# The end of a two-block transformer kernel: the last residual addition done by accumulating transfers into DRAM

## The chip, the cores and the metric

The kernel runs on one core of a Trainium2 chip. The metric is device time in microseconds (us) of one execution. A core has five engines that run their own instruction streams and meet only at semaphores: TensorE (PE, matrix products into PSUM banks), VectorE (DVE) and ScalarE (ACT) for elementwise work, GpSimd (POOL), and SyncE (SP), which here only issues transfers (DMAs). A DMA moves data between DRAM and the on-chip memory SBUF. It can be issued by SP, ACT or POOL, and is carried out by 16 DMA engines that all of them share.

## The reference

Two blocks run one after the other on a sequence of 512 tokens with 1024 channels. What matters here is the very end of the second block, the feed-forward part:

```python
def reference(x, ...):
    x = first_block(x, ...)
    return second_block(x, ...)

def second_block(x, ...):
    h = x
    for l in range(DEPTH_2):            # one layer
        a = rms_norm(h, ln_mix_pre[l])
        ...                             # four mixers side by side
        mix = jnp.concatenate([y_a, y_b, y_c, y_d], axis=-1) @ w_out[l]
        h = h + rms_norm(mix, ln_mix_post[l])

        a = rms_norm(h, ln_ffn_pre[l])
        ff = (jax.nn.silu(a @ w_ffn_gate[l]) * (a @ w_ffn_up[l])) @ w_ffn_down[l]
        h = h + rms_norm(ff, ln_ffn_post[l])
    return h
```

The output is `h + rms_norm(ff, ...)`: a residual `h` that is known before the feed-forward part begins, plus `ff` scaled by one number per token and one per channel.

## The kernel before, in words

Activations lie transposed: channels on the 128 partitions, in 8 tiles `k` of 128 channels, and the 512 tokens along each row. `X` holds the residual (128 x 8 x 512, f32, 2 MB), `Y` the output of the last product. Every product is done in three f32 passes (high and low halves of weights and activations), so PE is busy nearly all the time: weights stream from DRAM in units of up to 512 KB (SP, `load`, L1308), ACT makes their high half (`high`, L1321), DVE their low half (`low`, L1327), PE multiplies (L1446 to L1448).

The last stage is `feed_forward` (L3786). Its parts run in this order on PE: the output product of the mixers, gate/up product of the first half of the hidden channels, down product of that half, then the same two for the second half. The first product is followed by the norm object `mixed`, the last by `final`; both are of the class `RmsPost` (L1071). `mixed` computes `X = X + norm(Y)` and the halves for the next product; it ends with X holding the last residual `h`. `final` computes `X = X + norm(Y)` again, which is the output.

How `RmsPost` works for `final`. As each block of the down product is added into `Y` (`block`, and L336), ACT squares it (L1121), and POOL sums the squares (L1128, L1131). The last of the 8 blocks is computed in two halves of 256 tokens (`in_halves`, L1462): PE finishes the first half and increments the semaphore `half`, then does the second half and increments `unit_used`. Between its last products PE forms the mean of the squares of each token with a matrix of constants (L1091, L1097), and ACT turns it into the inverse root, by a logarithm and an exponential (L268, L269), in the tile `line[INV]`, whose semaphore `inv` reaches 2 when the first half of the tokens is done and 4 with the second.

DVE runs `dve_last` (L1172). `norm(i)` is two instructions: Y times channel gain times inverse root (L1187, scalar_tensor_tensor), and X plus that (L1189, tensor_tensor). The items `i` of `final` are 13 pieces: 5 tiles of the first 256 tokens, 5 of the second, and 3 tiles of all 512 tokens. DVE does the first half of block 8 (L1177), waits for `inv` 2, does two items, then `whole()` (a wait for PE to end), the second half of block 8 (L1177), and the rest, with a wait for `inv` 4 before item 5. ACT needs that second L1177 for the square that the second half's inverse root begins with.

The output is stored by `store` (L1215): for every item a wait for its addition, and one DMA from X to `out`, the even items by SP and the odd ones by ACT. Each then waits for its own transfers to land, and the program ends.

Of the kernel before, what the change touches and what calls it, by code (L numbers as in the profile page):

```python
# [10 lines left out]
ALU = mybir.AluOpType  # L11
# [4 lines left out]
T = 512  # L16
# [183 lines left out]
class Stage:  # L200
# [34 lines left out]
    def block(self, pool=None):  # L235


        block = self.ctx.enter_context(self.nc.Block(no_gpsimd_drain=True))
        self.cleared, self.core.to_clear = self.core.to_clear, []

        @block.gpsimd
        def _(eng):
            nums = sorted(h.num for h in self.cleared)
            while nums:
                n = 1
                while n < len(nums) and nums[n] == nums[0] + n:
                    n += 1
                eng.sem_clear(range(nums[0], nums[0] + n))
                nums = nums[n:]
            if pool:  # L250
                pool(eng)
        return block
# [569 lines left out]
class LayerNorm:  # L822
# [106 lines left out]
    def pool(self, gp):  # L929
        core, s, Y, line = self.core, self.s, self.core.Y, self.core.line  # L930
        self.tile_ready(gp, 1)
        done(gp, gp.tensor_tensor(line[SUM][:], Y[:, 0, :], Y[:, 1, :], ALU.add), s.sum)  # L932
        gp.wait_ge(s.sq, 2)
        done(gp, gp.tensor_tensor(line[SSUM][:], line[SQ0][:], line[SQ1][:], ALU.add), s.ssum)
        for k in range(2, KD - 1):
            self.tile_ready(gp, k)
            done(gp, gp.tensor_tensor(line[SUM][:], line[SUM][:], Y[:, k, :], ALU.add), s.sum)
            gp.wait_ge(s.sq, k + 1)
            done(gp, gp.tensor_tensor(line[SSUM][:], line[SSUM][:], line[(SQ0, SQ1)[k % 2]][:], ALU.add), s.ssum)
# [131 lines left out]
class RmsPost:  # L1071
# [100 lines left out]
    def dve_last(self, dve, evac, whole, split):  # L1172
        core, s, X, Y, line = self.core, self.s, self.core.X, self.core.Y, self.core.line

        def block(h):
            i, cols = self.b0 + KD - 1 + h, HALVES[h]
            dve.tensor_tensor(Y[:, KD - 1, cols], Y[:, KD - 1, cols], core.bank(i)[:, cols], ALU.add).then_inc(core.freed(i), 1)  # L1177

        def low(i):
            k, cols = self.items[i]  # L1180
            dve.wait_ge(s.src_hi, i + 1)
            dve.scalar_tensor_tensor(self.xl[:, k, cols], X[:, k, cols], core.param(self.pre, k), self.xh[:, k, cols].bitcast(F32),  # L1182
                                     ALU.mult, ALU.subtract).then_inc(s.src_lo, 1)

        def norm(i):
            k, cols = self.items[i]
            dve.scalar_tensor_tensor(Y[:, k, cols], Y[:, k, cols], core.param(self.post, k), line[INV][:, cols], ALU.mult, ALU.mult).then_inc(s.normed, 1)  # L1187
            dve.wait_ge(s.normed, i + 1)
            dve.tensor_tensor(X[:, k, cols], X[:, k, cols], Y[:, k, cols], ALU.add).then_inc(s.x, 1)  # L1189

        if self.restored:
            dve.wait_ge(self.restored, 16)
        dve.wait_ge(s.half, 1)
        if isinstance(evac, Accumulate):
            block(0)
        split()
        dve.wait_ge(s.inv, 2)
        begun = 3 if self.late else 2
        for i in range(begun):
            norm(i)  # L1200
            if self.late and i:
                low(i - 1)
        whole()
        if isinstance(evac, Accumulate):
            block(1)
        for i in range(begun, len(self.items)):
            if self.items[i] == (0, HALVES[1]):
                dve.wait_ge(s.inv, 4)
            norm(i)
            if self.late:  # L1210
                low(i - 1)
        if self.late:
            low(len(self.items) - 1)

    def store(self, eng, odd, sem):  # L1215
        out = self.core.io["out"].rearrange("p (k t) -> p k t", t=T)
        for i in range(odd, len(self.items), 2):
            k, cols = self.items[i]
            eng.wait_ge(self.s.x, i + 1)
            eng.dma_start(out[:, k, cols], self.core.X[:, k, cols]).then_inc(sem, 16)  # L1220
        eng.wait_ge(sem, 16 * len(range(odd, len(self.items), 2)))

# [2561 lines left out]
def feed_forward(core):  # L3786


    with Stage(core, "ffn") as st:
        x, h = core.source, core.hidden[FT]  # L3790
        s = st.sems("restored stored_sp stored_act")
        mixed = RmsPost(core, st, "a", "post", x, "fpre", restored=s.restored)
        final = RmsPost(core, st, "b", "fpost")
        parts = [Product(core, st, "out_", KD, (KD,), [(KD, Plain(core.Y))], Split(st, core.Y, x), mixed)]
        for half in range(2):
            up = Gated(*h, mixed)
            parts.append(Product(core, st, f"gateup{half}_", 2 * FT, (KD,), [(2 * FT, up)], mixed if half == 0 else Hidden(x)))
            out = Plain(core.Y) if half == 0 else Accumulate(core.Y)
            parts.append(Product(core, st, f"down{half}_", KD, (6, 5), [(KD, out)], Hidden(h, up.s.hidden_lo), final if half else None))

        def pool(gp):
            mixed.pool(gp)
            final.pool(gp)

        def restore(act):
            act.dma_start(core.X[:], core.io["kept"].rearrange("p (k t) -> p k t", t=T)).then_inc(s.restored, 16)

        def sync(sp):
            final.store(sp, 0, s.stored_sp)

        def scalar_last(act):
            final.store(act, 1, s.stored_act)

        Chain(core, st, parts).run(st, pool=pool, sync=sync, scalar_first=restore, scalar_last=scalar_last)


def program(nc, io):
    with ExitStack() as ctx:
        core = Core(nc, io, ctx)
        for n, kts, blocks in STREAMS:  # L3820
            for i in range(blocks * len(kts)):
                kt = kts[i % len(kts)]
                core.stream.append((io[n][i][:, 0:kt * P], kt))
        place = lambda n, shape, at: nc.alloc_sbuf_tensor_at(n, shape, F32, offset=at)
        Z, O = place("Z1", [P, 27, T], Z1_AT), place("O", [P, KD, T], LINE_AT(4))
        small, norm = core.Y[:, 4:7, :], place("rwkv_norm", [P, 4, T], LINE_AT(0))
        gate = place("rwkv_gate", [P, 4, T], end_of("W") - 4 * TILE)

        AR = place("rwkv_AR", [P, 4, NCH, 2, C], at_of("S"))
        elast = place("rwkv_elast", [P, 4, NCH], at_of("H") + 4 * TILE)  # L3830
        load_and_project(core, Z, O, small, norm, gate, AR, elast)
        rwkv(core, Z, O, gate, AR, elast)
        first_layers(core, O)
        dilated_layer(core)
        Z, gates = place("Z2", [P, 16, T], at_of("H")), place("gates", [P, 1, T], LINE_AT(INV))
        made = LateInputs(core)
        second_layers(core, Z, gates, made)
        late_mixers(core, Z, gates[:, 0, :], made)
        feed_forward(core)
# [112 lines left out]
```

## Time and profile before

| | us |
|---|---|
| median of 3 runs (lowest, highest) | 2152.04 (2150.08, 2152.43) |
| the profiled execution's own time | 2155.46 |
| its span, first to last instruction | 2153.7 |
| PE busy / DVE busy / ACT busy / POOL busy | 2078.1 / 1233.9 / 822.8 / 274.2 |

The profiled execution was 3.4 us longer than the median of the timed runs; 1.8 us of its time lie outside its span. PE is busy 96% of the span, at a granted clock of 0.991 of full speed. An engine's busy time does not tell what the end waits for: for a change at the very end, the instructions of the last 20 us have to be read in order, engine by engine. In rows of the timeline the first number is the start of an instruction in us, the second its duration.

### The profile page before, as it was taken

The page shows a single profiled execution, that of the slowest core. Times are in us where ns is not written, and L with a number is a line of the kernel's source. Part 1 is how long each engine was busy: PE and PEld are TensorE (multiplying, and loading weights), DVE is VectorE, ACT ScalarE, POOL GpSimd, SP SyncE. Part 2 cuts the span into 40 slices and gives each one's busy share as a digit, 9 for nine tenths or more (in the row PEclk, how much of TensorE's full clock was granted, in tenths as well). Part 3 has the DMA queues.
Part 4 walks back from the last instruction along what each step waited for, and adds up shares of the span by engine and source line. Part 5 has one row for each costly group of instructions (what it writes and reads, how often), then busy time and mean ns, then how long its engine had stood idle before and what let it go on. Part 6 is the DMA issues. An engine that isn't in the chain of part 4 may idle for free. (4 is left out here: it accounts for less than half of the span.)

```text
span 2153.7 us, 31656 instructions
## 1 busy us (share of the span) xinstructions
PE 2078.1 (96%) x12976; PEld 1680.8 (78%) x12976; DVE 1233.9 (57%) x1760; ACT 822.8 (38%) x1317; POOL 274.2 (13%) x262
## 2 busy tenths in 40 slices
PE   8999989999999999999999999999998899999997
PEld 6876868888888878888888888886665578888886
DVE  5558866642444676667473553467678647533544
ACT  4343234531332534444462332353234554322322
POOL 0000003000002100000301870030542010000001
PEclk9999999999999999999999999999999999999999
DMA  6220003333223222222123222223111042233322
GB/s 234 69 71 27 4 3 108 98 98 98 90 96 98 70 93 74 69 71 77 59 88 103 89 98 98 98 93 122 59 59 36 2 147 88 91 90 114 98 81 66
DMA packets 52400, 179.29 MB, mean 83 GB/s; under 512 B 5864, under 2 KB 7144, under 8 KB 52000
## 3 DMA queue, kind: packets, MB, share of 16 engines
q1 hardware_dynamic: 48144, 165.58, 23.7%
q10 hardware_dynamic: 3616, 8.00, 1.1%
q0 software_dynamic: 496, 3.69, 0.4%
q8 instruction: 103, 1.69, 0.3%
q14 instruction: 41, 0.34, 0.1%
HBM read 172.51 MB, written 4.21 MB: 82 GB/s over the span
## 5 line engine op out<-in xcount | busy, mean ns | idle before, releaser
L1332 DVE TENSOR_TENSOR w_lo<-w_raw,w_hi 128x1024 fp32r<-128x1024 f32 (+1 forms) x320 | 402.6, 1260 | 664.1 <-ACT w_hi L1325 657.2
L1325 ACT ACTIVATE w_hi<-w_raw 128x1024 fp32r<-128x1024 f32 (+1 forms) x320 | 328.9, 1031 | 800.3 <-PE banks L1448 744.2
L1446 PE MATMUL banks<-xh,w_hi 128*128 128x512 f32 x1544 | 617.6, 400 | 3.6 <-PEq L214 2.6
L1448 PE MATMUL banks<-xh,w_lo 128*128 128x512 f32 x1544 | 603.7, 391 | 0.0
L1447 PE MATMUL banks<-xl,w_hi 128*128 128x512 f32 x1544 | 603.2, 391 | 0.0
L1446 PEld LDWEIGHTS banks<-xh,w_hi 128*128 128x128 f32 x1544 | 291.1, 189 | 73.3 <-issue 13.1
L1448 PEld LDWEIGHTS banks<-xh,w_lo 128*128 128x128 f32 x1544 | 290.5, 188 | 62.0
L1447 PEld LDWEIGHTS banks<-xl,w_hi 128*128 128x128 f32 x1544 | 291.2, 189 | 57.4 <-issue 1.2
L1446 PE MATMUL banks<-hh,w_hi 128*128 128x512 f32 x653 | 255.2, 391 | 1.0 <-DVE hl L372 1.0
L1447 PE MATMUL banks<-hl,w_hi 128*128 128x512 f32 x653 | 254.4, 390 | 0.0
L1448 PE MATMUL banks<-hh,w_lo 128*128 128x512 f32 x653 | 254.3, 389 | 0.0
L1446 PEld LDWEIGHTS banks<-hh,w_hi 128*128 128x128 f32 x653 | 122.6, 188 | 27.3 <-DVE hl L372 1.4
L1447 PEld LDWEIGHTS banks<-hl,w_hi 128*128 128x128 f32 x653 | 122.6, 188 | 25.8 <-issue 0.5
L1448 PEld LDWEIGHTS banks<-hh,w_lo 128*128 128x128 f32 x653 | 122.6, 188 | 25.4
L932 POOL TENSOR_TENSOR line<-Y 128x512 f32<-128x512 f32 x4 | 5.2, 1294 | 1068.6 <-DVE Y L915 1068.6
L1128 POOL TENSOR_TENSOR line<-line,line 128x512 f32<-128x512 f32 x2 | 2.6, 1290 | 421.0 <-ACT line L1121 421.0
L1507 PE MATMUL banks<-xh,w_hi 128*128 128x256 f32 (+1 forms) x165 | 53.3, 339 | 1.8 <-ACT xh L961 1.3
L1508 PE MATMUL banks<-xh,w_lo 128*128 128x256 f32 (+1 forms) x165 | 52.1, 332 | 0.0
L372 DVE TENSOR_TENSOR hl<-line,hh 128x512 fp32r<-128x512 f32 x64 | 48.4, 757 | 2.2
L369 DVE TENSOR_TENSOR line<-line 128x512 f32<-128x512 f32 x64 | 48.3, 755 | 0.0
L361 ACT ACTIVATE hh<-line 128x512 fp32r<-128x512 f32 x64 | 40.6, 635 | 2.0
L1514 PE MATMUL banks<-xl,w_hi 128*128 128x256 f32 (+1 forms) x165 | 39.7, 349 | 1.5 <-DVE xl L1029 0.6
(540 smaller groups left out, 2770.2 us busy)
## 6 DMA issues: line engine op xcount, KB each, us to landing
w_raw<-in_w SPq DMA_DIRECT2D x128, 512.0 KB, 3.5
w_raw<-in_w_gu SPq DMA_DIRECT2D x44, 512.0 KB, 3.5
w_raw<-in_w_c_in SPq DMA_DIRECT2D x40, 512.0 KB, 3.5
w_raw<-in_w_ab_in SPq DMA_DIRECT2D x27, 512.0 KB, 3.5
w_raw<-in_w_in SPq DMA_DIRECT2D x25, 512.0 KB, 3.4
w_raw<-in_w_down SPq DMA_DIRECT2D x16, 384.0 KB, 3.1
w_raw<-in_w_down SPq DMA_DIRECT2D x16, 320.0 KB, 2.8
w_raw<-in_w_ab_out SPq DMA_DIRECT2D x8, 512.0 KB, 3.5
```

Of the source, the lines that this page charges most:

```text
L361: act.activation(self.hh[:, b, :], relu[:], ACT.Square).then_inc(self.s.hidden_hi, 1)
L369: dve.tensor_tensor(sq[:], relu[:], relu[:], ALU.mult).then_inc(self.s.squared, 1)
L372: dve.tensor_tensor(self.hl[:, b, :], sq[:], self.hh[:, b, :].bitcast(F32), ALU.subtract).then_inc(self.s.hidden_lo, 1)
L932: done(gp, gp.tensor_tensor(line[SUM][:], Y[:, 0, :], Y[:, 1, :], ALU.add), s.sum)
L1325: act.activation(core.w_hi[u % SLOTS][:, 0:n], core.raw[u % RAW][:, 0:n], ACT.Copy).then_inc(core.hi_ready, 1)
L1332: dve.tensor_tensor(lo[:, 0:n], core.raw[u % RAW][:, 0:n], hi[:, 0:n].bitcast(F32), ALU.subtract).then_inc(core.split_ready, 1)
L1446: pe.matmul(bank, hi[:, w], src.xh[:, kk, :], start=kk == 0, stop=False)
L1447: pe.matmul(bank, hi[:, w], src.xl[:, kk, :], start=False, stop=False)
L1448: mm = pe.matmul(bank, lo[:, w], src.xh[:, kk, :], start=False, stop=last)
L1507: pe.matmul(banks[i][:, cols], hi[:, w], src.xh[:, k, cols], start=n == 0, stop=False, skip_group_check=True)
L1508: pe.matmul(banks[i][:, cols], lo[:, w], src.xh[:, k, cols], start=False, stop=False, skip_group_check=True)
L1514: mm = pe.matmul(banks[i][:, cols], hi[:, w], src.xl[:, k, cols], start=False, stop=last, skip_group_check=True)
```

## The change

`mixed`, the norm in front of the feed-forward products, now has a `store` too: once all its items are added (X holds the last residual), POOL issues one transfer of the whole of X, 2 MB, to `out`. At the end, `norm(i)` of `final` is only the scaling L1187; the addition L1189 is left out. For every item POOL waits until it is scaled and issues a DMA from Y to `out` with `accum_op=ALU.add`: the transfer adds Y to what lies in DRAM. `final.add` first waits for the earlier store (`stored`), and at the end for all 13 transfers. SP and ACT store nothing. In `dve_last` the wait `whole()` and the second half of block 8 now come before all items of `final`, in place of after two.

```diff
         def norm(i):
             k, cols = self.items[i]
             dve.scalar_tensor_tensor(Y[:, k, cols], ...).then_inc(s.normed, 1)
-            dve.wait_ge(s.normed, i + 1)
-            dve.tensor_tensor(X[:, k, cols], X[:, k, cols], Y[:, k, cols], ALU.add).then_inc(s.x, 1)
+            if self.late:
+                dve.wait_ge(s.normed, i + 1)
+                dve.tensor_tensor(X[:, k, cols], X[:, k, cols], Y[:, k, cols], ALU.add).then_inc(s.x, 1)
...
         split()
+        if not self.late:
+            whole()
+            block(1)
         dve.wait_ge(s.inv, 2)
-        begun = 3 if self.late else 2
+        begun = 3 if self.late else 0
...
-        whole()
-        if isinstance(evac, Accumulate):
-            block(1)
+        if self.late:
+            whole()
...
-    def store(self, eng, odd, sem):
+    def store(self, gp, sem):
         out = self.core.io["out"].rearrange("p (k t) -> p k t", t=T)
-        for i in range(odd, len(self.items), 2):
-            k, cols = self.items[i]
-            eng.wait_ge(self.s.x, i + 1)
-            eng.dma_start(out[:, k, cols], self.core.X[:, k, cols]).then_inc(sem, 16)
-        eng.wait_ge(sem, 16 * len(range(odd, len(self.items), 2)))
+        gp.wait_ge(self.s.x, len(self.items))
+        gp.dma_start(out, self.core.X[:]).then_inc(sem, 16)
+
+    def add(self, gp, stored, sem):
+        out = self.core.io["out"].rearrange("p (k t) -> p k t", t=T)
+        gp.wait_ge(stored, 16)
+        for i, (k, cols) in enumerate(self.items):
+            gp.wait_ge(self.s.normed, i + 1)
+            gp.dma_start(out[:, k, cols], self.core.Y[:, k, cols], accum_op=ALU.add).then_inc(sem, 16)
+        gp.wait_ge(sem, 16 * len(self.items))
...
         def pool(gp):
             mixed.pool(gp)
+            mixed.store(gp, s.stored)
             final.pool(gp)
+            final.add(gp, s.stored, s.added)
...
-        Chain(core, st, parts).run(st, pool=pool, sync=sync, scalar_first=restore, scalar_last=scalar_last)
+        Chain(core, st, parts).run(st, pool=pool, scalar_first=restore)
```

The end of DVE's stream before, from the last whole block of the down product (L336) on; the first L1177 is the first half of block 8, line_56 is the inverse root:

```order
L336 TENSOR_TENSOR Y<-Y,banks 128x512
L1177 TENSOR_TENSOR Y<-Y,banks 128x256
L1187 SCALAR_TENSOR_TENSOR Y<-Y,params,line_56 128x256
L1189 TENSOR_TENSOR X<-X,Y 128x256
L1187 SCALAR_TENSOR_TENSOR Y<-Y,params,line_56 128x256
L1189 TENSOR_TENSOR X<-X,Y 128x256
L1177 TENSOR_TENSOR Y<-Y,banks 128x256
L1187 SCALAR_TENSOR_TENSOR Y<-Y,params,line_56 128x256
L1189 TENSOR_TENSOR X<-X,Y 128x256
```

And now, to the end of the program:

```order
L336 TENSOR_TENSOR Y<-Y,banks 128x512
L1177 TENSOR_TENSOR Y<-Y,banks 128x256 x2
L1187 SCALAR_TENSOR_TENSOR Y<-Y,params,line_56 128x256 x10
L1187 SCALAR_TENSOR_TENSOR Y<-Y,params,line_56 128x512 x3
L214 UNCONDITIONAL_BRANCH
```

All 13 additions are gone, and the second L1177 moved ahead of the first scaling. The end of POOL's stream before, from the last sum of squares for `mixed` on:

```order
L1131 TENSOR_TENSOR line_60<-line_60,line_57 128x512
L1128 TENSOR_TENSOR line_60<-line_57,line_58 128x512
L1131 TENSOR_TENSOR line_60<-line_60,line_57 128x512
L1131 TENSOR_TENSOR line_60<-line_60,line_58 128x512
L1131 TENSOR_TENSOR line_60<-line_60,line_57 128x512
L1131 TENSOR_TENSOR line_60<-line_60,line_58 128x512
L1131 TENSOR_TENSOR line_60<-line_60,line_57 128x512
L214 UNCONDITIONAL_BRANCH
```

And now:

```order
L1131 TENSOR_TENSOR line_60<-line_60,line_57 128x512
L1223 DMA out_x<-X 128x4096
L1128 TENSOR_TENSOR line_60<-line_57,line_58 128x512
L1131 TENSOR_TENSOR line_60<-line_60,line_57 128x512
L1131 TENSOR_TENSOR line_60<-line_60,line_58 128x512
L1131 TENSOR_TENSOR line_60<-line_60,line_57 128x512
L1131 TENSOR_TENSOR line_60<-line_60,line_58 128x512
L1131 TENSOR_TENSOR line_60<-line_60,line_57 128x512
L1232 DMA out_x<-Y 128x256 x10
L1232 DMA out_x<-Y 128x512 x3
L214 UNCONDITIONAL_BRANCH
```

POOL gained the store of the whole residual (L1223) between its two groups of sums, and 13 DMAs in a row at the end; SP lost its 7 and ACT its 6.

## Rows read from the trace of the kernel before

**Rows 1.** The end of the chain that ended last: start, duration, engine, tile, line.

```profile
2137.59 0.42 ACT line L269
...
2138.04 0.50 DVE Y L1187
...
2138.56 0.42 DVE X L1189
...
2150.48 0.69 DVE X L1189
```

**Rows 2.** Groups of DVE instructions, 2138 to 2151.3 us: count | busy us, mean ns.

```profile
L1187 DVE SCALAR_TENSOR_TENSOR Y<-Y,params,line 128x256 f32<-128x256 f32 x10 | 4.8, 479 | 2.4 <-ACT line L269 2.4
L1189 DVE TENSOR_TENSOR X<-X,Y 128x256 f32<-128x256 f32 x10 | 4.2, 425 | 0.3
L1187 DVE SCALAR_TENSOR_TENSOR Y<-Y,params,line 128x512 f32<-128x512 f32 x3 | 2.2, 746 | 0.0
L1189 DVE TENSOR_TENSOR X<-X,Y 128x512 f32<-128x512 f32 x3 | 2.1, 692 | 0.1
```

**Rows 3.** Timeline of SP, last store: start and duration of the issue.

```profile
2151.20 0.33 SPq L1220 DMA_DIRECT2D out_x<-X  x1
```

**Rows 4.** Timeline of PE: last product of each half of block 8.

```profile
2134.83 0.28 PE L1474 MATMUL banks<-hh,w_lo 128*128 128x256 f32 x1
...
2137.47 0.28 PE L1474 MATMUL banks<-hh,w_lo 128*128 128x256 f32 x1
```

**Rows 5.** Timeline of DVE: both halves of block 8, and scaling after them.

```profile
2135.22 0.42 DVE L1177 TENSOR_TENSOR Y<-Y,banks 128x256 f32<-128x256 f32 x1 [5.43 <-PE banks L1474]
...
2139.76 0.41 DVE L1177 TENSOR_TENSOR Y<-Y,banks 128x256 f32<-128x256 f32 x1
2140.09 0.48 DVE L1187 SCALAR_TENSOR_TENSOR Y<-Y,params,line 128x256 f32<-128x256 f32 x1
```

**Rows 6.** Timeline of ACT: end of the second half's inverse root.

```profile
2142.05 0.42 ACT L269 ACTIVATE line<-line 128x256 f32<-128x256 f32 x1
```

**Rows 7.** Timeline of DVE at `mixed`: independent scalings one behind the other.

```profile
1773.39 0.48 DVE L1182 SCALAR_TENSOR_TENSOR xl<-X,params,xh 128x256 fp32r<-128x256 f32 x1
1773.79 0.48 DVE L1187 SCALAR_TENSOR_TENSOR Y<-Y,params,line 128x256 f32<-128x256 f32 x1
...
1782.75 0.74 DVE L1182 SCALAR_TENSOR_TENSOR xl<-X,params,xh 128x512 fp32r<-128x512 f32 x1
1783.41 0.74 DVE L1187 SCALAR_TENSOR_TENSOR Y<-Y,params,line 128x512 f32<-128x512 f32 x1
```

**Rows 8.** Timeline of POOL: the only four DMAs it issues.

```profile
1.26 0.76 POOL L3671 DMA_DIRECT2D params<-in_params  x1 [0.82 <-POOLq L3942]
...
12.65 0.55 POOL L3676 DMA_DIRECT2D consts<-in_consts  x1 [10.43 <-DMA X<-in_x]
13.19 0.53 POOL L3677 DMA_DIRECT2D load_masks<-in_masks  x1
...
25.08 0.53 POOL L3680 DMA_DIRECT2D Y<-in_small  x1 [0.30 <-POOL masks L3679]
```

**Rows 9.** DMA issues: engine, count, KB each, median us from issue to landing.

```profile
w_raw<-in_w SPq DMA_DIRECT2D x128, 512.0 KB, 3.5
...
w_raw<-in_w_down SPq DMA_DIRECT2D x16, 384.0 KB, 3.1
...
X<-kept ACTq DMA_DIRECT2D x1, 2048.0 KB, 9.3
...
Y<-in_small POOLq DMA_DIRECT2D x1, 768.0 KB, 4.7
...
out_x<-X SPq DMA_DIRECT2D x2, 256.0 KB, 2.0
```

**Rows 10.** Busy time by stretch; the last two numbers: DMA share, GB/s.

```profile
2138.00:2151.20 13.20, 1.01 (x4) 0.30 (x2) 12.69 (x27) 1.31 (x4) 0.00 (x0) 0.69 0.38 135
2151.20:2153.70 2.50, 0.00 (x0) 0.00 (x0) 0.00 (x0) 0.00 (x0) 0.00 (x0) 0.50 0.34 127
```

**Rows 11.** Timeline of SP, first store of the output.

```profile
2139.01 0.34 SPq L1220 DMA_DIRECT2D out_x<-X  x1
```

**Rows 12.** Around the end of `mixed`: last addition (DVE), weight load (SP), its use (ACT).

```profile
1788.29 0.69 DVE L1189 TENSOR_TENSOR X<-X,Y 128x512 f32<-128x512 f32 x1
...
1792.50 0.33 SPq L1313 DMA_DIRECT2D w_raw<-in_w_gu  x1
...
1807.34 2.00 ACT L1325 ACTIVATE w_hi<-w_raw 128x1024 fp32r<-128x1024 f32 x2
```

**Rows 13.** Timeline of DVE beside two of POOL's issues.

```profile
11.88 2.52 DVE L1246 TENSOR_TENSOR xl<-X,xh 128x512 fp32r<-128x512 f32 x4
```

More of the change, by code:

```diff
@@ L1196, in dve_last @@
         split()
+        if not self.late:
+            whole()
+            block(1)
         dve.wait_ge(s.inv, 2)
-        begun = 3 if self.late else 2
+        begun = 3 if self.late else 0
         for i in range(begun):
             norm(i)
-            if self.late and i:
+            if i:
                 low(i - 1)
-        whole()
-        if isinstance(evac, Accumulate):
-            block(1)
+        if self.late:
+            whole()
         for i in range(begun, len(self.items)):
@@ L3790, in feed_forward @@
         x, h = core.source, core.hidden[FT]
-        s = st.sems("restored stored_sp stored_act")
+        s = st.sems("restored stored added")
         mixed = RmsPost(core, st, "a", "post", x, "fpre", restored=s.restored)
@@ L3802, in pool @@
             mixed.pool(gp)
+            mixed.store(gp, s.stored)
             final.pool(gp)
+            final.add(gp, s.stored, s.added)
         def restore(act):
             act.dma_start(core.X[:], core.io["kept"].rearrange("p (k t) -> p k t", t=T)).then_inc(s.restored, 16)
[L3808 to L3812, printed above, removed]
-        Chain(core, st, parts).run(st, pool=pool, sync=sync, scalar_first=restore, scalar_last=scalar_last)
+        Chain(core, st, parts).run(st, pool=pool, scalar_first=restore)
 def program(nc, io):
```

## The prediction

> **What bounds the kernel now.** I read the page's busy times first: PE is at 96% of the span, so anything done beside its stream is free, and only what comes after its last product can move the end. The chain of waits names what that is. From the end of ACT's inverse root (2137.59 + 0.42 = 2138.01 us) the chain is VectorE alone, scaling and addition in turn, to 2150.48 + 0.69 = 2151.17 [rows 1]. The groups of that stretch give the sizes: ten scalings of 256 columns at 479 ns and three of 512 at 746 ns, ten additions at 425 ns and three at 692 ns, 6.3 us of additions in all [rows 2]. After the last addition comes one store: issued at 2151.20, and the span ends at 2153.7, so 2.50 us from issue to end [rows 3]. Those 2.50 us are 2.0 us of landing [rows 9] and 0.5 us for the engines to meet.
>
> **VectorE's part, without the additions.** The second half of block 8 now waits for PE before anything is scaled. In the first half DVE began 0.11 us after PE's last product ended (2134.83 + 0.28 = 2135.11, then 2135.22) [rows 4, 5]. The second half's last product ends at 2137.47 + 0.28 = 2137.75, so L1177 starts at 2137.86, and the first scaling 0.33 us behind it (2139.76 to 2140.09) [rows 5], at 2138.19. Before it was 2138.04: the move costs 0.15 us. For what it gives back: from the start of that L1177 to the end of the second inverse root were 2139.76 to 2142.05 + 0.42 = 2142.47, 2.71 us [rows 5, 6]. Now it ends at 2137.86 + 2.71 = 2140.57, and item 5 can start at 2140.60.
>
> Scalings that do not need each other follow one another closer than their durations say: 0.40 us for 256 columns (1773.39 to 1773.79) and 0.66 us for 512 (1782.75 to 1783.41) [rows 7]. Items 0 to 4 start from 2138.19 to 2139.79. DVE then waits until 2140.60 (0.4 us, a new wait; behind it stand only the other items). Items 5 to 9 start from 2140.60 to 2142.20, items 10 to 12 at 2142.60, 2143.26 and 2143.92, and DVE ends at 2144.67: 6.5 us earlier than 2151.17. That much is nearly certain. It is worth only what the transfers behind it let through.
>
> **GpSimd's part.** The 13 transfers are issued by one engine, where two took turns. The trace has four DMAs issued by POOL, at 0.76, 0.55, 0.53 and 0.53 us of POOL's time each, and the two that stand back to back have no gap [rows 8]. None of them adds. At 0.55 us, first issue at 2138.19 + 0.48 + 0.08 = 2138.75 (an item's duration, and a little to pass the semaphore), the last of 13 starts 12 x 0.55 = 6.60 us later, at 2145.35, after its item is ready at 2144.67: POOL would set the pace, not DVE. For the landing: SP's loads took 3.1 us for 384 KB and 3.5 for 512 KB, so some 4.3 for 768 KB; POOL's load of 768 KB took 4.7 [rows 9]. A transfer of POOL's lands 0.4 us later. End: 2145.35 + 2.50 + 0.4 = 2148.25, which is 5.45 us less than 2153.7. This is the lower bound: an adding transfer as cheap as a plain one.
>
> **The transfers themselves.** An addition in DRAM has to read what is there, as well as Y, before it writes. No such transfer is in the trace. The nearest rows are the plain stores of the same 2.1 MB: DMA share 0.38 over 13.20 us and 0.34 over 2.50 us, together 5.87 us of all 16 engines' time, or 357 GB/s while they work [rows 10]. The bounds are then 5.87 us (the second read is free) and 17.6 us (three passes, each at a full transfer's price). I take twice, 11.7 us, one pass for each operand read. The transfers then bind and POOL's pace is hidden. A 256 KB store lands in 2.0 us [rows 9], of which 0.73 is data at 357 GB/s, so 1.27 is fixed, 1.67 for POOL. Sum: 2138.75 + 1.67 + 11.74 + 0.5 = 2152.66, which is 1.0 us less than 2153.7. Of the 6.5 us that DVE gives back, 5.5 go into transfers that run at half speed.
>
> The Trainium skill, page "Collectives: The Full Stack", section "The bandwidth ceiling: the fold count and why AG ≠ RS ≠ AR", says that an adding transfer needs two source reads on one read ring and so runs at about half a copy's speed (it gives a ratio of 1.93). By that figure the data would take 5.87 x 1.93 = 11.3 us and the span end at 2152.3 (estimate from that page). No row of this trace shows it, and the sum above does not need it.
>
> **The early store.** POOL issues it when the last addition of `mixed` has ended, at 1788.29 + 0.69 = 1788.98. It is one issue on an idle engine; behind it on POOL stand only the sums for `final`, which begin when the last down product does. The 2 MB go beside the weight stream. A load of the same size took 9.3 us beside it [rows 9]. The weight load issued at 1792.50 is used by ACT at 1807.34, 14.84 us later, and takes 3.5 us: 11.3 us of slack [rows 9, 12], more than the 9.3 us by which the store could hold it up. I cost it at nothing. Were the cover gone, PE would stand a few us, once. X is not written any more afterwards, so there is no wait for `stored` at the end, and the 13 stores that SP and ACT lose were off DVE's path except the last [rows 3, 11].
>
> **Rivals.** (A) *Adding is nearly free.* POOL's issues or the landings bind. For it: 13 small transfers, 16 engines that stood idle more than half of the time. Time from -5.45 us (above) to -2.9 us, the latter with issues of 0.76 us, the longest of the four [rows 8]: last start 2138.75 + 9.12 = 2147.87, end 2150.77. On the median that is 2146.6 to 2149.1.
>
> (B) *The forecast*, -1.0 us: 2151.0.
>
> (C) *POOL is held up a little more.* An adding transfer needs twice the descriptors, so 2 x 0.55 = 1.10 us of POOL each: last start 2138.75 + 13.20 = 2151.95, end 2151.95 + 2.9 + 0.73 (one more pass over 256 KB) = 2155.58, +1.9 us. In the same size class is that POOL cannot write descriptors while DVE scales: first issue at 2144.75, last at 2151.35, end 2154.25, or +0.6. Against that one: beside the issues at 12.65 and 13.19 DVE ran additions on two SBUF inputs, and they took 0.55 and 0.53 us, no longer than the one at 25.08 [rows 8, 13].
>
> The Trainium skill, page "SBUF — State Buffer", section "Who interferes with whom", tells of such a lock, but for VectorE's two-port modes and names copies, casts and tensor_scalar for them. The scaling here is none of these; no row shows POOL issuing beside one.
>
> (D) *It ends slower.* The mechanism is POOL's time for an adding issue, the place its queue of 13 at the end. With end = 2138.75 + 12 d + 3.63 the change loses from d = 0.94 us on, and is measurably slower from d = 1.30. Twice the longest row is 1.52 us: last start 2156.99, end 2160.6, +6.9 us. Three passes of the DMA engines lead to about the same place: 2138.75 + 1.67 + 17.6 + 0.5 = 2158.5, +4.8 us. For it: no row bounds an adding issue from above. Against it: the four issues differ little among themselves [rows 8]. Time 2156.8 to 2159.
>
> **How the numbers follow.** The differences were made against the profiled execution (span 2153.7, own time 2155.46, 1.76 outside). It stands 3.4 us above the median of 2152.04; the end of the program after PE is the same in both, so I apply the differences to the median. About 0.2%, 4.3 us, is what a measurement of this kernel can tell from no change. Chances: A 0.30, B 0.36, C 0.13, D 0.21. The forecast is B, 2151.0 us. Of A some 0.23 lies beyond 4.3 us; of D nearly all does, and 0.02 to 0.03 of other losses come on top, such as an early store that is not hidden after all. So faster 0.23, same 0.54, slower 0.23. The range has to reach well into A and D: 2146.4 to 2157.5. B's own range, with a second read between 0.8 and 1.2 of the first, is 2149.9 to 2152.2.
>
> **What the new profile would show.** The last scaling of DVE ends near 2144.7 (if PE ends where it did), with a wait of 0.4 us before item 5: that tests the first step. The duration of POOL's issues L1232 tests C and D: near 0.55 us, and starts 0.55 us apart, if they are like the rows. The time from POOL's last issue to the end tests the transfers: about 2.9 us if adding is free, 7 us if they lag behind at half speed; the busy share of the DMA engines over the tail, 5.9 or 11.7 us, says the same. PE's idle time around 1790 to 1810 should stay nothing. The forecast is wrong if issues take over 0.94 us, or if the last landing comes within 3 us of the last issue.

## The result, and the profile after

The change makes the kernel slower. Over 18 executions of each, the changed kernel has a median of 2153.94 us and the kernel before 2150.16; the ratio is 1.0020, with a 95% interval of 1.0013 to 1.0027. The medians differ by 3.8 us (the ratio gives 4.3) where I had forecast 1.0 us less. The time stayed inside the stated range, the direction was wrong.

The profiled execution of the changed kernel has a span of 2153.0 us (own time 2154.8), shorter than that of the kernel before. That is no contradiction, and it is the first thing to sort out: PE ended its last product earlier in this execution. The rows of PE's last product and of DVE and POOL behind it, from three timelines (start, duration):

```profile
2133.13 0.28 PE L1486 MATMUL banks<-hh,w_lo 128*128 128x256 f32 x1
```

```profile
2130.87 0.42 DVE L1177 TENSOR_TENSOR Y<-Y,banks 128x256 f32<-128x256 f32 x1 [5.42 <-PE banks L1486]
2133.44 0.42 DVE L1177 TENSOR_TENSOR Y<-Y,banks 128x256 f32<-128x256 f32 x1 [2.16 <-PE banks L1486]
2133.78 2.06 DVE L1187 SCALAR_TENSOR_TENSOR Y<-Y,params,line 128x256 f32<-128x256 f32 x5
2136.19 4.06 DVE L1187 SCALAR_TENSOR_TENSOR Y<-Y,params,line 128x256 f32<-128x256 f32 x8 [0.35 <-ACT line L269]
```

```profile
2134.86 11.65 POOL L1232 DMA_DIRECT2D out_x<-Y  x13 [7.18 <-DVE Y L1187]
...
2141.44 5.06 POOL L1232 DMA_DIRECT2D out_x<-Y  x1
```

PE ends at 2133.13 + 0.28 = 2133.41, where it ended at 2137.75 before [rows 4]. Among the profiles of this study that end lies between 2131.9 and 2137.75, in kernels whose work up to there is the same, so spans of single executions say nothing of the tail. I compare the tail from here on: from the end of PE's last product to the end of the span. It was 2153.7 - 2137.75 = 15.95 us, and is now 2153.0 - 2133.41 = 19.59 us: 3.6 us more, which is the 3.8 us of the medians. Measured from the first L1177 instead, 2153.7 - 2135.22 = 18.48 [rows 5] against 2153.0 - 2130.87 = 22.13, it is the same 3.65.

DVE does what was forecast. It starts scaling 0.37 us after PE's end, waits 0.35 us before item 5, and ends at 2136.19 + 4.06 = 2140.25, 6.84 us after PE's end; it was 13.42 us before [rows 1, 4]. The 6.6 us are gained on DVE and lost behind it. POOL's last issue starts at 2141.44, so the 13 issues start (2141.44 - 2134.86) / 12 = 0.55 us apart, as the four in the trace of before had suggested [rows 8]. But from that last issue to the end of the span are 11.6 us.

The DMA engines are what is left. The tail's row of the busy times by stretch, with the shares that answer to [rows 10] (last two numbers: DMA share, GB/s), and the landing times (KB each, us):

```profile
2133.30:2153.00 19.70, 1.36 (x5) 0.55 (x4) 6.45 (x14) 1.66 (x4) 11.65 (x13) 0.65 0.81 106
```

```profile
out_x<-Y POOLq DMA_DIRECT2D x10, 128.0 KB, 5.3
...
out_x<-Y POOLq DMA_DIRECT2D x3, 256.0 KB, 9.7
```

The engines were busy 0.81 x 19.7 = 15.96 us for 2.1 MB that took them 5.9 us as plain stores. In the stretches of 2 us between 2138 and 2150 their share is 1.03 or more, at 139 to 163 GB/s. The share adds up the recorded durations of the packets and divides by 16 engines; above 1 the durations on one engine overlap, so "busy time" here and below is a sum of packet times. The 256 KB pieces land 9.7 us after their issue (2.0 before [rows 9]): they queue. The durations of POOL's issues are a trap here. They are 0.93 to 5.06 us and overlap, yet the starts are 0.55 us apart. Without the add they are 0.54 us (plain13, below), so the long ones go with the transfers that queue behind them and not with a slow POOL; what POOL does in that time no row shows.

### The profile page after: what moved, and what is told of

It is laid out like the page before. It is cut to its first block and busy times, and to the rows that moved or that the text cites. A ratio compares the mean times of both kernels' runs of the same rounds, so it can differ in the third digit from the quotient of the medians.

```text
span 2153.0 us, 31643 instructions
## 1 busy us (share of the span) xinstructions
PE 2078.5 (97%) x12976; PEld 1681.2 (78%) x12976; DVE 1227.2 (57%) x1747; ACT 822.7 (38%) x1317; POOL 287.4 (13%) x276
## 3 DMA queue, kind: packets, MB, share of 16 engines
HBM read 172.51 MB, written 6.31 MB: 83 GB/s over the span
## 5 line engine op out<-in xcount | busy, mean ns | idle before, releaser
L1458 PEld LDWEIGHTS banks<-xh,w_hi 128*128 128x128 f32 x1544 | 291.1, 189 | 73.5 <-issue 13.1
```

The lines of the kernel that those rows point to most:

```text
L1458: pe.matmul(bank, hi[:, w], src.xh[:, kk, :], start=kk == 0, stop=False)
```

## The experiments

Theory 1: an adding transfer takes the DMA engines 2.7 times as long as a plain one, and that alone binds the end. Theory 2: POOL's path is slow. Theory 3: it is the reading of the destination in DRAM. The tail of each run is counted from the end of PE's last product of block 8, as above. Where a run was timed once only, I read its profile and claim nothing from its time.

**The add left out (plain13).**

```diff
-            gp.dma_start(out[:, k, cols], self.core.Y[:, k, cols], accum_op=ALU.add).then_inc(sem, 16)
+            gp.dma_start(out[:, k, cols], self.core.Y[:, k, cols]).then_inc(sem, 16)
```

> This kernel leaves out the addition of the residual at the end: the 13 transfers that POOL issues are the same, from Y to the output, but plain stores. Theory 1 (the adding transfer itself is dear, 2.5 to 2.7 times a plain one in time of the DMA engines): without the add POOL's spacing of 0.54 us sets the pace; from PE's last product to the end of the span 1.5 + 12 x 0.54 + 2.9 = 10.9 us, where the kernel before has 15.95 and the changed one 19.7; time 5 us (0.23%) below before; DMA busy share of the tail adds up to 6 us. Theory 2 (POOL's queue is slow, its issues last up to 5 us because its descriptors are slow to be taken): about as the changed kernel, 19 us from PE's end, 4 us above before, and issues that still overlap up to several us.

Ratio 0.9988 (0.9978 to 0.9997), span 2147.0. POOL's issues (duration min/median/max, first and last start), the tail's busy times, and the landings:

```profile
L1232 POOL DMA_DIRECT2D out_x<-Y x13: 539/539/586, 2137.2 to 2143.6; - x13
```

```profile
2135.70:2147.00 11.30, 1.33 (x5) 0.52 (x4) 6.46 (x14) 1.63 (x4) 6.96 (x13) 0.76 0.52 186
```

```profile
out_x<-Y POOLq DMA_DIRECT2D x10, 128.0 KB, 2.2
out_x<-Y POOLq DMA_DIRECT2D x3, 256.0 KB, 2.8
```

PE's end was 2135.78, so the tail is 11.2 us (forecast 10.9); the DMA engines are busy 0.52 x 11.3 = 5.9 us; POOL's issues are 0.54 us each, one behind the other, and no longer overlap. The same instructions on the same engine without the add are 8.4 us shorter at the end: theory 2 falls. (Its output lacks the residual.) It is also what the change would have given had adding been free, 0.12% (2.6 us) against the kernel before in its timing, with an interval up to 0.22%, and 4.7 us by the tails of the two profiles.

**Two plain passes (plain_twice).**

```diff
+            gp.dma_start(out[:, k, cols], self.core.Y[:, k, cols]).then_inc(sem, 16)
+            gp.dma_start(kept[:, k, cols], self.core.Y[:, k, cols]).then_inc(sem, 16)
...
```

> This kernel leaves out the addition of the residual at the end: each of the 13 pieces of Y is stored plainly twice by POOL, once to the output and once to a scratch tensor in DRAM, 4.2 MB in 26 transfers. It asks what two passes cost without an adder. Theory 1a (an add costs its two reads, each like one plain pass): DMA busy time of the tail 12 us, and POOL's 26 issues at 0.54 us take 14 us, so 1.5 + 13.5 + 2.9 = 17.9 us from PE's end. Theory 1b (an adding transfer costs more than two passes): the busy time here is 12 us too, but the 16 us of the changed kernel are then more than that, so reads alone do not explain it. Theory 2 (POOL's queue is slow): busy time well above 12 us, near 30.

```profile
2132.70:2151.50 18.80, 1.28 (x5) 0.47 (x4) 6.46 (x14) 1.58 (x4) 13.85 (x26) 0.62 0.63 223
```

Each piece goes once to the output and once to a scratch tensor in DRAM. Two plain passes of the same bytes in the same pieces keep the DMA engines busy 0.63 x 18.8 = 11.8 us, twice 5.9, as my forecast took for the add. The tail of 18.8 us is set by POOL's 26 issues here. So an adding transfer in these pieces costs 4.1 us more than two whole passes (theory 1b).

**Adding into SBUF (acc_sbuf).**

```diff
-            gp.dma_start(out[:, k, cols], self.core.Y[:, k, cols], accum_op=ALU.add).then_inc(sem, 16)
+            gp.dma_start(self.core.X[:, k, cols], self.core.Y[:, k, cols], accum_op=ALU.add).then_inc(sem, 16)
```

> The 13 adding transfers go from Y into X in SBUF instead of the output in DRAM, so the output holds only the residual; all else is as in the changed kernel. Theory 1 (the cost lies in the DMA engines, whatever the destination): DMA busy time of the tail stays near 16 us and the tail near 19.5 us from PE's end. Theory 3 (the cost is the reading of the destination in DRAM): busy time falls to 8 to 12 us, and the end comes 4 to 7 us earlier.

```profile
2135.80:2153.50 17.70, 1.29 (x5) 0.48 (x4) 6.46 (x14) 1.59 (x4) 11.73 (x13) 0.65 0.78 119
```

Busy 0.78 x 17.7 = 13.8 us, tail 17.7 us: 2.2 us less than with the output in DRAM. Neither theory's number came out (16, or 8 to 12); both have a part. With the destination in SBUF 2.2 us of the 10.1 that adding costs over a plain store into DRAM are gone; 7.9 us remain without any reading of DRAM. What a plain transfer of these pieces from SBUF to SBUF takes was not measured, so how much of the 13.8 us is the adding is not shown. One execution each; the two executions of hybrid5 below, with the same adding transfers, agree to 0.1 us (0.67 x 13.9 and 0.67 x 13.8).

**Row length (late_2048, late_512, late_256).** POOL waits for all items, and then adds all of Y in rows of 2048, 512 or 256 elements per partition:

```diff
-        for i, (k, cols) in enumerate(self.items):
-            gp.wait_ge(self.s.normed, i + 1)
-            gp.dma_start(out[:, k, cols], self.core.Y[:, k, cols], accum_op=ALU.add).then_inc(sem, 16)
+        gp.wait_ge(self.s.normed, len(self.items))
+        for at in range(0, KD * T, 2048):
+            gp.dma_start(self.core.io["out"][:, at:at + 2048], self.core.Y.rearrange("p k t -> p (k t)")[:, at:at + 2048], accum_op=ALU.add).then_inc(sem, 16)
...
```

> POOL waits until all 13 items are scaled and then issues two adding transfers with rows of 2048 elements (8 KB) in place of 13 with rows of 256 or 512: 256 rows instead of 1664. Theory 1, cost by the byte: data time of 14.5 us again, so from the first issue to the end 14.5 + 1.7 + 0.5 to 1.5 = 17 to 18 us, and an end 6 us later than the changed kernel since it starts 6 to 7 us later. Rival, cost by the row (a fixed delay for each read and write back): data time falls well below 10 us, towards 6, and the end comes no later than in the changed kernel.

> As in late_2048, POOL waits until all items are scaled and then issues all of Y as adding transfers, but eight of them with rows of 512 elements (2 KB): 1024 rows. The DMA busy time of the tail was 15.75 us in the changed kernel (1664 rows), 10.85 in late_2048 (256 rows). Theory by byte and row: a straight line through these two, 56 ns of one DMA engine for every row (4.9 us x 16 / 1408): 10.85 + 768 x 0.0557 / 16 = 13.5 us. Rival, that the number of transfers or their beginning beside VectorE's work made the difference and not the rows: about 10.9 us.

> The same with sixteen adding transfers of rows of 256 elements (1 KB): 2048 rows. By byte and row: 10.85 + 1792 x 0.0557 / 16 = 17.1 us of DMA busy time. By number of transfers (16, against 13 in the changed kernel and 2 in late_2048): near 16.9, so this one alone does not tell them apart, but with late_512 (8 transfers: 13.5 by rows, and by transfers 10.85 + 6 x 0.445 = 13.5 as well) the line is either straight in both or not; if only the start beside VectorE counted: 10.9.

The tails' busy times of the three kernels, in this order:

```profile
2134.80:2155.50 20.70, 1.33 (x5) 0.53 (x4) 6.46 (x14) 1.64 (x4) 1.83 (x2) 0.64 0.53 101
```

```profile
2135.90:2158.90 23.00, 1.31 (x5) 0.51 (x4) 6.46 (x14) 1.62 (x4) 7.19 (x8) 0.62 0.57 91
```

```profile
2134.10:2159.20 25.10, 1.29 (x5) 0.49 (x4) 6.46 (x14) 1.60 (x4) 14.32 (x16) 0.61 0.67 84
```

| kernel | rows, KB each | DMA busy us | forecast |
|---|---|---|---|
| late_2048 | 256, 8 KB | 0.53 x 20.7 = 11.0 | |
| late_512 | 1024, 2 KB | 0.57 x 23.0 = 13.1 | 13.5 |
| changed kernel | 1664, 1 and 2 KB | 16.0 | |
| late_256 | 2048, 1 KB | 0.67 x 25.1 = 16.8 | 17.1 |
| plain13 (no add) | 1664 | 5.9 | |

The busy time grows with the rows: (13.1 - 11.0) x 16 / 768 = 44 ns of one engine for each row, then (16.8 - 13.1) x 16 / 1024 = 58 ns. With rows of 8 KB the add costs 11.0 / 5.9 = 1.9 plain passes, which is the doubling I had forecast; with rows of 1 to 2 KB 2.7. What these runs exclude is that the start beside VectorE made the difference, since nothing runs beside them. They don't separate rows from the number of transfers, since every transfer has 128 rows; the records of single packets, below, do so in part. Neither theory of late_2048 gave its data time (14.5 us, or well below 10). My expectation that its end comes 6 us later than in the changed kernel was off too: its tail is 2155.5 - 2134.88 = 20.6 us, only 1.0 us more. Its first issue comes 2142.33 - 2134.88 = 7.45 us after PE's end against 1.45, 6.0 us later, and the longer rows give back 16.0 - 11.0 = 5.0 of them.

**What the packets show.** The trace keeps every packet of the DMA engines with its size and duration. Of an adding transfer each row is one packet; of POOL's plain transfers a packet is 4 KB, so plain13 does not have the 1664 short packets that the changed kernel has. POOL's queue over the whole execution, changed kernel first, plain13 second (packets, MB, share), differs by 1664 - 512 = 1152 packets for the same bytes:

```profile
q0 software_dynamic: 2512, 7.88, 1.4%
```

```profile
q0 software_dynamic: 1360, 7.88, 1.0%
```

The plain stores by SP and ACT in the kernel before do have one packet for each row of 1 or 2 KB, so they are what to compare with. From the records behind PE's end, the usual duration being the median:

| kernel | rows | usual row | rows over 40 ns longer | what longer rows add |
|---|---|---|---|---|
| kernel before (plain) | 1664 | 46 ns (1 KB), 85 (2 KB) | 0 | 0 us |
| changed kernel | 1664 | 102 ns (1 KB), 178 (2 KB) | 191 | 3.1 us |
| late_256 | 2048 | 102 ns (1 KB) | 210 | 3.4 us |
| late_512 | 1024 | 178 ns (2 KB) | 70 | 1.6 us |
| late_2048 | 256 | 629 ns (8 KB) | 22 | 0.9 us |
| acc_sbuf | 1664 | 111 ns (1 KB), 187 (2 KB) | 19 | 0.1 us |

Two things add up, then. The usual adding row takes twice the plain row and 8 to 10 ns more: 102 against 2 x 46, 178 against 2 x 85. By the rows of 1 and 2 KB it is 26 ns and 76 ns for each KB, which gives 634 ns for 8 KB (629 measured); both sizes stand in one kernel, so this part goes by the row and not by the number of transfers. And about one row in nine (191 of 1664) takes much longer, up to 2.3 us. Among these tails such rows are frequent only where the adding transfer goes to DRAM. Having almost none of them makes acc_sbuf 3.0 us shorter than the changed kernel; its usual rows, 9 ns slower, take 0.9 of that back. Why the long rows occur, and whether their number goes by rows, transfers or time, stays open. So the 44 and 58 ns for each row above are no fixed cost: between 8 KB and 1 KB the usual rows explain 3.0 of 5.9 us and the long ones 2.5.

These are sums of packet durations. The time from the first packet to the end of the last is 16.0 us in the changed kernel, 11.0 in late_2048, 13.3 in late_512 and 15.4 in late_256, where the sum is 16.9: durations overlap there by 1.5 us or more, so how much of a long row's duration really holds up its engine is not shown.

**The early store (early_store).** The kernel before with this store; SP and ACT also wait for it before their stores at the end:

```diff
             mixed.pool(gp)
+            mixed.early(gp, s.stored)    # waits for X, then gp.dma_start(out, self.core.X[:])
```

> The kernel before, with the early store of the residual by POOL added and its end otherwise as it was (13 additions on VectorE, 13 plain stores, which now also wait for the early store, long done). My account: the store is hidden beside the weight stream, the time is that of the kernel before within 0.1%, PE shows no idle time around 1790 to 1810 us. Rival: the 2 MB hold up the weights; then PE waits there and the time is 1 to 4 us longer, and part of the change's loss is here.

Ratio 0.9997 (0.9988 to 1.0006). Busy times of 20 us behind the store, of the kernel before first, of this one second:

```profile
1790.00:1810.00 20.00, 20.00 (x88) 16.07 (x87) 13.12 (x14) 9.00 (x11) 0.00 (x0) 1.00 0.24 79
```

```profile
1790.00:1810.00 20.00, 20.00 (x88) 16.10 (x87) 13.84 (x16) 7.93 (x11) 0.00 (x0) 1.00 0.41 145
```

The DMA engines carry nearly twice as much there, and PE is busy throughout in both. (In this execution the store began at 1785.6, so the row misses its first part; PE was busy without a gap from 1785 to 1789 as well.) The tail is 2148.5 - 2132.60 = 15.9 us, as before. The early store is free, and no part of the loss.

**The order alone (reorder).** The kernel before, with `whole()` and `block(1)` ahead of the items of `final`:

> The kernel before with only the order changed: the wait for PE's end and the second half of block 8 ahead of all items of the final norm, all additions and stores as before. VectorE's first scaling comes 0.15 us later, item 5 does not wait (the second inverse root is ready 2.85 us after PE's end, item 5 comes at 4.7 us), so the tail from PE's end is 15.95 + 0.15 - 0.1 = 16.0 us. Rival: the early second half costs more, 0.5 us or above, because scaling begins later than the sum says.

```profile
2135.49 0.42 DVE L1177 TENSOR_TENSOR Y<-Y,banks 128x256 f32<-128x256 f32 x1 [2.16 <-PE banks L1476]
2135.83 0.48 DVE L1187 SCALAR_TENSOR_TENSOR Y<-Y,params,line 128x256 f32<-128x256 f32 x1
...
2147.93 0.69 DVE L1189 TENSOR_TENSOR X<-X,Y 128x512 f32<-128x512 f32 x1
```

PE ended at 2135.45: tail 2151.1 - 2135.45 = 15.6 us, against 15.95. The move costs nothing; 0.3 us less in one execution I don't claim as a gain.

**Fewer adding transfers (hybrid5, hybrid8).** The first 5 (or 8) items are added by POOL's transfers, the rest by DVE and stored plainly by SP and ACT:

```diff
+ADDED = 5
...
-            if self.late:
+            if self.late or i >= ADDED:
                 dve.wait_ge(s.normed, i + 1)
                 dve.tensor_tensor(X[:, k, cols], X[:, k, cols], Y[:, k, cols], ALU.add).then_inc(s.x, 1)
...
-        for i, (k, cols) in enumerate(self.items):
+        for i, (k, cols) in enumerate(self.items[:ADDED]):
...
+    def store_rest(self, eng, odd, sem, stored):
+        mine = range(ADDED + odd, len(self.items), 2)
...
```

> Early store as in the changed kernel; the first 5 items (first 256 tokens of 5 tiles, 640 KB) go as adding transfers by POOL, the other 8 are added by VectorE and stored plainly by SP and ACT. VectorE ends 5 x 0.43 us earlier than in the kernel before, and the adding transfers, some 4.6 us of the DMA engines' time from 2.9 us after PE's end on, finish before the last plain store: from PE's end 11.3 + 2.5 = 13.8 us, 2.1 us less than the 15.95 of the kernel before (0.1% faster). If adding transfers hold up the plain stores behind them in the DMA engines, the end is set by the last landing: 15 to 16 us, no gain. If what costs is not the amount of data that is added but the path through POOL itself (its issues, its landing): as the changed kernel, 19 us.

> hybrid5 a second time, since its interval reached 1.0001. By the tails of the two profiles (13.9 us from PE's end against 15.95) the ratio is 0.9990; an interval wholly below 1 would bear that out, one around 1 would leave the gain seen in the profile alone.

> As hybrid5, with 8 of the 13 items as adding transfers. VectorE would end 1.2 us earlier than in hybrid5 (2133.0 + 9.9), but the DMA engines get more adding work: 1024 rows of 1 KB, by the runs with rows of 1 KB 8.4 us of busy time (half of 16.8), and 2.9 us of plain stores, 11.3 us from 2.9 us after PE's end. If the engines' time for adding is what costs, the engines now bind: 14.2 us, and 1.0 to 1.5 us of landing and end, so 15.2 to 15.7 us from PE's end, longer than hybrid5 (13.9) though VectorE does less. If VectorE still binds: 12.6 us.

The tails of hybrid5 and of hybrid8, then DVE's last instruction in each:

```profile
2133.00:2146.90 13.90, 1.31 (x5) 0.50 (x4) 10.65 (x22) 1.61 (x4) 4.49 (x5) 0.67 0.67 151
```

```profile
2131.80:2146.70 14.90, 1.32 (x5) 0.52 (x4) 9.38 (x19) 1.63 (x4) 7.20 (x8) 0.65 0.76 141
```

```profile
2143.68 0.69 DVE L1191 TENSOR_TENSOR X<-X,Y 128x512 f32<-128x512 f32 x1
```

```profile
2141.12 0.69 DVE L1191 TENSOR_TENSOR X<-X,Y 128x512 f32<-128x512 f32 x1
```

hybrid5: ratio 0.9992 (0.9983 to 1.0001), and the second time 0.9989 (0.9981 to 0.9998); tails of 13.8 us in both, 2.1 us less than before, as forecast. Here DVE binds: its last addition ends at 2144.37, 2.5 us before the end, the same 2.5 us as in the kernel before [rows 3]. hybrid8: DVE ends 9.9 us after PE, 1.4 us sooner than in hybrid5, and the tail is 14.8 us, 1.0 us longer (forecast 15.2 to 15.7), though still 1.1 us below that of the kernel before; from DVE's end at 2141.81 to the end of the span are 4.9 us. The engines bind, busy 0.76 x 14.9 = 11.3 us as forecast. hybrid5 is faster than the kernel before by 0.1%, at the edge of what the timing resolves. It was not timed beside the changed kernel; by the tails it is 5.7 us shorter.

**GpSimd as the adder (pool_adds).** The kernel before, with items 1, 3, 5, 7 and 9 added by POOL in SBUF:

```diff
...
+            gp.tensor_tensor(self.core.X[:, k, cols], self.core.X[:, k, cols], self.core.Y[:, k, cols], ALU.add).then_inc(by_pool, 1)
...
```

> The kernel before, with five of its 13 additions (items 1, 3, 5, 7 and 9, 128x256 each) done by GpSimd as tensor_tensor in SBUF in place of VectorE; no early store, no adding transfer, all stores by SP and ACT as before. VectorE's chain loses 5 x 0.43 = 2.15 us, GpSimd needs 0.65 us for each (half of the 1.29 us of its 512 columns) and has 1.3 us for it: from PE's end 15.95 - 2.15 = 13.8 us, 0.1% faster, about what hybrid5 gives, without the DMA engines' extra time. Rival: the two engines get in each other's way over SBUF, both reading two inputs; then the scalings or GpSimd's additions stretch beyond 0.48 and 0.65 us and the gain is below 1 us.

Ratio 1.0002 (0.9994 to 1.0011): no gain. The tail is 2149.9 - 2134.28 = 15.6 us, where I expected 13.8. The groups of its tail (count, busy us, mean ns), and one of POOL's additions with DVE's beside it:

```profile
L1188 DVE SCALAR_TENSOR_TENSOR Y<-Y,params,line 128x256 f32<-128x256 f32 x10 | 4.9, 518 | 2.4 <-ACT line L269 2.4
L1221 POOL TENSOR_TENSOR X<-X,Y 128x256 f32<-128x256 f32 x5 | 4.6, 916 | 11.0 <-DVE Y L1188 11.0
L1191 DVE TENSOR_TENSOR X<-X,Y 128x256 f32<-128x256 f32 x5 | 3.3, 667 | 0.2
```

```profile
2137.98 0.90 POOL L1221 TENSOR_TENSOR X<-X,Y 128x256 f32<-128x256 f32 x1 [1.21 <-DVE Y L1188]
```

```profile
2138.33 0.83 DVE L1191 TENSOR_TENSOR X<-X,Y 128x256 f32<-128x256 f32 x1
```

The rival was right. DVE's additions of 256 columns take 667 ns in the mean where they took 425 [rows 2]. The mean mixes two kinds: two of the five stand beside no addition of POOL's and take 0.42 and 0.43 us, the three beside one 0.83. Each of POOL's five makes one instruction of DVE about 0.4 us longer (these three, one scaling of 0.90 us, one addition of 512 columns of 1.09), 2.0 us in all for the 2.15 that DVE no longer does. POOL's own take 916 ns where half of its 512-column time would be 650. The Trainium skill, page "SBUF — State Buffer", section "Who interferes with whom", says that a VectorE instruction with two SBUF inputs contends with a GpSimd instruction that reads SBUF; this trace agrees, 0.83 us against 0.42.

## Why the prediction was wrong

**VectorE's part** was right: the last scaling ends 6.84 us after PE (forecast 6.92), with the wait of 0.35 us before item 5 (0.4). The move of the second half cost nothing measurable in reorder (0.15 forecast).

**GpSimd's part** was right in the pace (0.55 us from start to start, which plain13 shows to be POOL's own) and low in the first issue. Item 0 is scaled at 2133.78 + 0.48 = 2134.26 and POOL starts at 2134.86, 0.60 us later, where I had put 0.08 from SP's example. From PE's end that is 1.45 us against 1.00: 0.45 us of the miss.

**The step that failed is the size of "The transfers themselves": "I take twice, 11.7 us, one pass for each operand read."** The mechanism was the one forecast, the transfers bind and hide POOL's pace; the term measured 15.96 us, 4.2 us more. With it the sum closes: forecast -1.0, + 4.2 for the data, + 0.45 for the first issue = +3.6 us, which is what the tails show (19.59 - 15.95). Everything between first issue and end that is not data was 18.14 - 15.96 = 2.2 us, as forecast (1.67 + 0.5).

What the runs showed in its place: two passes would have taken 11.8 us (plain_twice), and the adding rows take more than two plain rows each. The packets took 16.0 us from the first to the last as well. By their durations, of the 4.2 us some 1.0 is the 8 to 10 ns by which the usual adding row exceeds two plain ones, and 3.1 are the 191 rows that took much longer. With rows of 8 KB both are small and the doubling nearly holds (11.0 us). Why some rows into DRAM take so long is open, and their durations may overlap with others, so the larger part of the miss is located in the long rows but not explained. I had the two bounds, 5.9 and 17.6, and took the middle because it had a mechanism; nothing in the rows spoke for the middle over the upper half, and the pieces' size should have counted for it. Rival D named three passes as one way to the slower side and gave +4.8 us; that it came near (2.7 plain passes) does not show three passes, and its other mechanism, POOL's time per issue, played no part. A is excluded by the 16.0 us of data, C by issues that start 0.55 us apart while VectorE is still scaling.

The Trainium skill's figure of half a copy's speed (page "Collectives: The Full Stack", section "The bandwidth ceiling: the fold count and why AG ≠ RS ≠ AR") is a ratio of 1.93 measured there on a collective among four ranks. The run of 8 KB rows agrees, 1.9. For the rows of this kernel the measurement is 2.7, and the measurement decides.

**The early store** cost nothing, as forecast (0.9997).

## What to carry to other kernels

Moving an addition from an engine into a transfer trades a few hundred ns of that engine for DMA time: here 0.43 us of VectorE for 128 KB against about 1 us of all 16 DMA engines, where a plain store took 0.37. It pays most for as many pieces as the DMA engines can take while the compute engine is still the later of the two: tails of 15.95, 13.8, 14.8 and 19.6 us with 0, 5, 8 and 13 pieces. Long rows make the adding cheaper (11.0 us against 16.8), but no run here shows a gain from them, since late_2048 had to wait for all items. When two profiles differ by less than the main part varies from one execution to the next, compare the stretch behind a common event, not the spans.

## What was not expected of the hardware

- An adding transfer costs more in short rows: 2.1 MB took the DMA engines 11.0 us in rows of 8 KB, 13.1 in 2 KB and 16.8 in 1 KB, where plain stores in 1 and 2 KB rows took 5.9. Into SBUF the changed kernel's pieces took 13.8, into DRAM 16.0; into DRAM 191 of its 1664 rows took over 40 ns longer than usual, into SBUF 19.
- The usual adding row of 1, 2 or 8 KB took 102, 178 or 629 ns of one engine, a plain one of 1 or 2 KB 46 or 85; 7 to 11% of the rows added into DRAM took longer by over 40 ns, up to 2.3 us.
- The recorded durations of POOL's DMA issues grow when its transfers queue, from 0.54 to 5.06 us, and overlap; their starts stay 0.55 us apart.
- The page's count of DRAM traffic does not show the reads of the destination: with 2.1 MB added, read stays at 172.51 MB in both kernels. Only written grows, by the early store:

```profile
HBM read 172.51 MB, written 6.31 MB: 83 GB/s over the span
```

- Between the end of a VectorE instruction and a DMA issue of POOL's that waits for it lay 0.60 us, in plain13 as well; for SP it was 0.03 (2138.98 to 2139.01).
